# A two-layer hybrid decoder trunk on eight cores: mask, value products, MLP norm, squares and weight loads rearranged

## The reference

```python
def rmsnorm(x, g):
    y = xf * lax.rsqrt(jnp.mean(xf * xf, axis=-1, keepdims=True) + EPS)
    return (y * g.astype(jnp.float32)).astype(x.dtype)
...
        log_keep = jnp.where(mask, jax.nn.log_sigmoid(-z), 0.0)             # log(1 - beta)
        suffix = lax.cumsum(log_keep, axis=3, reverse=True) - log_keep      # sum over s<j<t
        weights = jnp.where(mask, jnp.exp(jax.nn.log_sigmoid(z) + suffix), 0.0)
        outs.append(jnp.einsum('bhqk,bhkd->bhqd', weights.astype(vb.dtype), vb))
...
    for layer in range(DEPTH):
        xn = rmsnorm(h, mix_norm_g[layer])
...
        h = h + mix
        hn = rmsnorm(h, mlp_norm_g[layer])
        h = h + jnp.square(jax.nn.relu(hn @ mlp_w1[layer])) @ mlp_w2[layer]
    return rmsnorm(h, final_norm_g)
```

## Time and profile before

| | us |
|---|---|
| median of 3 runs (lowest, highest) | 3104.32 (3099.47, 3390.04) |
| profiled execution: span of its slowest core | 3089.8 |
| spans of the 8 cores in it | 3069.8 to 3089.8 |
| PE busy, share | 2926.9, 95% |
| PE idle (span less busy) | 162.9 |
| DVE, ACT, POOL busy | 1410.4, 1412.3, 1179.8 |
| mean granted TensorE clock of the slowest core | 0.976 |

### The profile page before, as it was taken

The page is one execution under the profiler, slowest core; times in us unless marked ns, Lnnn a source line. Parts: engine busy times, 40 slices in busy tenths (PEclk is TensorE's granted clock), DMA queues, the critical chain, the costliest instruction groups (busy, mean ns, idle before and its releaser), DMA issues.

```text
span 3089.8 us, 46901 instructions; the slowest of 8 cores (3069.8 to 3089.8 us)
## 1 busy us (share of the span) xinstructions
PE 2926.9 (95%) x15157; PEld 1262.8 (41%) x15157; DVE 1410.4 (46%) x1671; ACT 1412.3 (46%) x2404; POOL 1179.8 (38%) x1685
## 2 busy tenths in 40 slices
PE   8999989999989999899998999998999989998998
PEld 3344433444433344333443444443444434443443
DVE  3410237552426445875644463333555574554002
ACT  2344243646345454356544345434554446353442
POOL 4211136343333444645443544333355435551110
PEclk9999999999999999999999999999999989999999
DMA  7788962554767998858664334465355495655222
GB/s 161 167 174 179 197 186 70 126 139 113 189 158 112 180 173 147 190 117 160 141 139 139 85 97 107 105 145 166 74 124 117 99 215 107 118 119 171 76 79 85
DMA packets 456925, 420.46 MB, mean 136 GB/s; under 512 B 310128, under 2 KB 334960, under 8 KB 456688
## 3 DMA queue, kind: packets, MB, share of 16 engines
q1 hardware_dynamic: 387424, 228.48, 32.9%
q0 software_dynamic: 69264, 188.99, 28.3%
HBM read 304.29 MB, written 89.13 MB: 127 GB/s over the span
## 4 chain that ended last, share of the span: by engine, by line
PE 80%; DVE 5%; DMA 5%; issue 3%; ACT 3%; POOL 2%; SPq 0%; DVEq 0%; ACTq 0%; POOLq 0%
PE ps L559 74%; PE ps L1282 3%; PE ps L1227 3%; DVE X_45 L674 1%; DMA Wk<-Wq 1%; DVE P L1243 1%; DMA stg<-xT 1%; DMA ring<-wblk 1%; PE ps L1231 1%; DMA h<-xT 1%; POOL ps_76 L943 1%; POOL ps_79 L943 1%; DMA oT<-stg 1%; POOL Wq L1257 1%; ACT L660 0%
## 5 line engine op out<-in xcount | busy, mean ns | idle before, releaser
L559 PE MATMUL ps<-X_45,ring 128*128 128x512 bf16 x4864 | 1118.9, 384 | 11.6 <-DVE X_45 L674 10.6
L549 ACT ACTIVATE ps<-ps 128x512 f32<-128x512 f32 (+3 forms) x832 | 576.5, 697 | 531.2 <-PE ps L559 322.5
L1257 POOL TENSOR_TENSOR Wq<-P 128x1022 bf16<-128x1022 f32 (+2 forms) x320 | 529.3, 1654 | 520.5 <-DVE P L1243 511.4
L559 PEld LDWEIGHTS ps<-X_45,ring 128*128 128x128 bf16 x4864 | 462.7, 99 | 575.9 <-issue 61.2
L1243 DVE TENSOR_TENSOR_SCAN P<-ps,carry,zeros 128x512 f32<-128x512 f32 x384 | 490.0, 1279 | 384.4 <-ACT ps L549 334.2
L559 PE MATMUL ps<-mix,ring 128*128 128x512 bf16 x2816 | 660.7, 380 | 3.6 <-DVE mix L914 2.7
L592 POOL DMA_DIRECT2D ring<-wbf x540 | 296.3, 551 | 764.9 <-PE ps L559 629.9
L715 DVE TENSOR_TENSOR h<-ps,h 128x512 f32<-128x512 f32 x384 | 263.1, 686 | 654.1 <-PE ps L559 652.3
L559 PE MATMUL ps<-ffB,ring 128*128 128x512 bf16 x2048 | 483.8, 379 | 0.0
L559 PEld LDWEIGHTS ps<-mix,ring 128*128 128x128 bf16 x2816 | 261.2, 98 | 315.4 <-issue 24.5
L1243 DVE TENSOR_TENSOR_SCAN P<-ps,zeros 128x128 f32<-128x128 f32 (+3 forms) x256 | 208.9, 820 | 375.9 <-ACT ps L549 361.7
(11 more groups left out here) (114 smaller groups left out, 1385.7 us busy)
## 6 DMA issues: line engine op xcount, KB each, us to landing
ring<-wbf POOLq DMA_DIRECT2D x540, 256.0 KB, 4.1
ring<-wblk POOLq DMA_DIRECT2D x180, 256.0 KB, 7.0
wbf<-ring SPq DMA_DIRECT2D x180, 256.0 KB, 5.7
stg<-xT SPq DMA_DIRECT2D x96, 256.0 KB, 5.4
h<-xT SPq DMA_DIRECT2D x64, 256.0 KB, 8.1
hsp<-h SPq DMA_DIRECT2D x64, 256.0 KB, 4.4
h<-hsp SPq DMA_DIRECT2D x64, 256.0 KB, 6.6
oT<-mixf SPq DMA_DIRECT2D x32, 256.0 KB, 7.6
```

The source lines that it names most:

```text
L549: return Req("act", lambda e: e.activation(out=out, in_=in_, func=func, **kw), reads, writes, dur, bias=bias)
L559: ins = pe.matmul(out, lhsT=l, rhs=r, start=(first and i == 0), stop=(last and i == n - 1), skip_group_check=True)
L1257: yield Req("pool", lambda e: e.tensor_tensor(out=W3[:, :, 0:w - 1], in0=P[:, :, 1:w], in1=P[:, :, 0:w - 1], op=ALU.subtract), [LP], [LWq] ...
```

## The change

In the code after, tensors and lines have moved: `X_45` is named `X_46`, and L559, L1227, L1282 are L588, L1349, L1402.

- **Mask.** The two mask matmuls go. The scan's second operation is max in place of add, and its second input is a floor: ones at masked places of the diagonal block, zeros elsewhere. Where the floor is one the running product stays one, and neighbouring differences are zero.
- **Value products.** Items are ordered so that four query blocks of one key chunk follow each other. Their transposes go into one buffer of 512 queries (two such buffers in place of seven small ones), and the value matmuls run once for the four: up to 512 columns each. P gets a column for the value that comes in from the right, filled by a small POOL instruction, and one subtraction makes all differences.
- **MLP norm.** `out_proj`'s result is written to X with the gain only, by DVE or ACT in turn. The sum of squares is taken aside (`rms_late`, power -1), and the second MLP matmul's result is multiplied by it on DVE and then added to h on POOL (on DVE for the last two rows of the last pass). Squared ReLU lets the scale pass as its square.
- **Squares in pairs.** Squares are written in float32 two rows at a time, a POOL or DVE add sums two rows into a bfloat16 one, and 4 ones matmuls do in place of 8.
- **Half of the first MLP matmul's squares** are made by POOL from a float32 copy in three `tmp` buffers, which frees the bank after the ReLU.
- **Weight loads** from `wbf` (540) are issued by SyncE, those from `wblk` (180) still by POOL.
- Also: three sets of conv and pool buffers in place of two, one conv step on ACT, U ahead of V in M, the gating scale and bias in one DVE instruction, `ms` buffers 4 for 2, other biases and slacks (PE no longer takes a chain's bias), attention paced at 0.4 and 0.6 of its rate in the input projections and around `out_proj` and the last second matmul, and a smaller scratch area for DMAs issued by POOL.

```diff
@@ _prep_weights, Builder.__init__, alloc
-    negq = np.where(k >= j, NEG, 0.0).astype(np.float32)
+    floor = (k >= j).astype(np.float32)
-        nc = self.nc = bass.Bass("TRN2", target_bir_lowering=False)
+        nc = self.nc = bass.Bass("TRN2", target_bir_lowering=False, dynamic_dma_scratch_size=4096)
-        self.Wk = sb("Wk", [128, NWT, 8, 128], BF16)
+        self.Wk = sb("Wk", [128, NG, 8, 512], BF16)
@@ Machine.run
-                    k = (st + f.bias + r.bias, f.n)
+                    k = (st + (r.bias if r.eng == "pe" else f.bias + r.bias), f.n)
@@ ring_fiber
-            yield Req("pool", (lambda slot, b, src: lambda e: e.dma_start(out=self.ring[:, slot, :], in_=src[b]))(slot, b, src),
+            yield Req("sp" if src is self.wbf else "pool",
+                      (lambda slot, b, src: lambda e: e.dma_start(out=self.ring[:, slot, :], in_=src[b]))(slot, b, src),
@@ new: square, rms; called by evac_x, evac_h, prefetch_x
+SQ = ((slice(0, 2), slice(2, 4), 0), (slice(4, 6), slice(6, 8), 4),
+      (slice(2, 4), slice(6, 8), 2), (slice(1, 4, 2), slice(5, 8, 2), 1))
+    def square(self, x, c, t, src, Ls, ev, eng="pool", slack=0.0):
...
+        if x == 2 and not odd:
+            yield Req("pool", lambda e: e.tensor_tensor(out=Xf[:, SQ[i][odd], hs], in0=sq, in1=sq, op=ALU.mult), Ls,
+                          [LX[k][t] for k in rows[odd]], 1.15, bias=0.5)
+        else:
+            r = self.act(Xf[:, SQ[i][odd], hs], sq, AF.Square, Ls, [LX[k][t] for k in rows[odd]], TT, False,
...
+        if odd:
+            yield lambda: c - 1 in ev.done
+            if i == 3 and x == 1:
+                eng = "dve"
+            yield Req(eng, lambda e: e.tensor_tensor(
+                out=X[:, SQ[i][2], t * TT:(t + 1) * TT].rearrange("p (a n) -> p a n", a=2),
+                in0=Xf[:, SQ[i][0], hs], in1=Xf[:, SQ[i][1], hs], op=ALU.add),
...
+    def rms(self, x, t, ev, power, parts=((0, 4),), bias=-0.05, slack=0.0):
...
+            rows = [SQ[i][2] for i in range(c0, c1)]
+            yield self.mm(self.bank(bk), [(self.cb[:, 0:128], X[:, k, ts]) for k in rows],
...
+        yield Req("act", lambda e: e.activation(out=m, in_=m, func=AF.Exp, scale=power), [], [self.Lms[ms]], 0.9)
+    def rms_late(self, t, ev):
+        self.r2[t] = yield from self.rms(2, t, ev, -1.0, bias=-0.01, slack=2.0)
@@ after out_proj: evac_x in place of evac_h and of norm_h
+            yield Req("dve", lambda e: e.tensor_tensor(out=self.h[:, c, ts], in0=self.bank(bk), in1=self.h[:, c, ts],
+                                                       op=ALU.add),
+                      [], [self.Lbank[bk], self.Lh[c][t]], 0.70)
             self.banks.free(bk)
-            if ev is not None:
-                yield self.act(self.X[1][:, c, ts], self.h[:, c, ts], AF.Square, [self.Lh[c][t]],
+            if c % 2:
+                yield Req("dve", lambda e: e.tensor_scalar(out=X[:, c, ts], in0=self.h[:, c, ts], scalar1=g, scalar2=None,
...
+            else:
+                yield Req("act", lambda e: e.activation(out=X[:, c, ts], in_=self.h[:, c, ts], func=AF.Copy, scale=g),
...
+            yield from self.square(2, c, t, self.h[:, c, ts], [self.Lh[c][t]], ev)
@@ evac_h, after the second MLP matmul
+            yield Req("dve", lambda e: e.tensor_tensor(out=self.tmp[:, b, :], in0=self.bank(bk), in1=self.ms[:, r2, :],
+                                                       op=ALU.mult),
+            self.banks.free(bk)
+            eng, d = ("dve", 0.70) if last and c >= 6 else ("pool", 1.15)
+            yield Req(eng, lambda e: e.tensor_tensor(out=self.h[:, c, ts], in0=self.tmp[:, b, :], in1=self.h[:, c, ts],
+                                                     op=ALU.add),
@@ mlp, evac1
+                if (j + t) % 2:
+                    yield self.act(m, ap, AF.Relu, [], [self.Lbank[bk], self.Ltmp[b]], TT, True)
+                    self.banks.free(bk)
+                    yield Req("pool", lambda e: e.tensor_tensor(out=F[:, jj, ts], in0=m, in1=m, op=ALU.mult),
@@ att_item
-            if first:
-                for h in range(2):
-                    ins = pe.matmul(zt[:, h * 512 + w - 128:h * 512 + w], lhsT=ident, rhs=negq, start=False, stop=True,
+        low = self.cb[:, 768 - w:768] if first else self.cb[:, 128:128 + w]
-                out=P[:, h, 0:w][:, ::-1], data0=zt[:, h * 512:h * 512 + w][:, ::-1], data1=self.zeros[:, 0:w],
-                initial=1.0 if first else self.carry[:, pv["cy"], h:h + 1], op0=ALU.mult, op1=ALU.add))(h),
+                out=P[:, h, 0:w][:, ::-1], data0=zt[:, h * 512:h * 512 + w][:, ::-1], data1=low[:, ::-1],
+                initial=1.0 if first else self.carry[:, pv["cy"], h:h + 1], op0=ALU.mult, op1=ALU.max))(h),
-        yield Req("pool", lambda e: e.tensor_tensor(out=W3[:, :, 0:w - 1], in0=P[:, :, 1:w], in1=P[:, :, 0:w - 1],
-        last = self.cf[:, 72:74] if first else self.carry[:, pv["cy"], :]
         yield Req("pool", lambda e: e.tensor_tensor(
-            out=W3[:, :, w - 1:w], in0=last.rearrange("p (h n) -> p h n", h=2), in1=P[:, :, w - 1:w], op=ALU.subtract),
+            out=W4, in0=P[:, :, 1:w + 1].rearrange("p h (j n) -> p h j n", n=128),
+            in1=P[:, :, 0:w].rearrange("p h (j n) -> p h j n", n=128), op=ALU.subtract), [LP], [LWq], w * 3.55e-3 + 0.05)
-                    ins = pe.matmul(av[h * 64:(h + 1) * 64, qc],
+        G["n"] += 1
+        if G["n"] == 4:
+                for j in range(4):
+                    q0 = j * 128 if first else 0
+                    for h in range(2):
+                        ins = pe.matmul(av[h * 64:(h + 1) * 64, q0:512],
```

442 lines of the change are left out of this document (255 added, 187 removed).

## The result

The changed kernel takes 2920.14 us (median; lowest 2914.97), the kernel before, beside it on the same chip, 3101.89 us. The ratio is 0.942, 95% interval 0.939 to 0.945: 5.8% faster, 180 us. The forecast was 2948 us.

The account below looks back on a forecast made before the run. PE bounds the kernel, busy 2926.9 of 3089.8 us. PE's work -96, waits and clock -82, new costs +22 make -156: from 3104 to 2948 us, 5% faster, range 2900 to 3000, chance 0.58.

Parts of the forecast that it names:

- PE's work, -96: Work taken from PE: value products -49 us, mask -15, ones matmuls -35, more entries into scores +3.
- Clock, -15: PE's granted clock, mean 0.976: with fewer gaps, 15 of at most 74 us lost to it come back.
- Waits that go, -67: PE's shortened waits: MLP norm 10 and 4 us, M stages 33, pool products 12, value products and scores 8.
- new ones, +22: Costs added beside PE's work: longer chain 7 us, full banks from POOL 10, late weight blocks 5.
- The MLP norm term: After `out_proj`: 10 of 11.6 us waited before `X_45,ring` go, and 4 of 16.5 before the ones matmuls.
- The longer chain, 7 us: Behind the last second-matmul group: one DVE step and a sum of rows add 1.4 us at four M starts and the end.
- POOL, 10 us: POOL's added adds, squares and sums: PE loses 10 us to full banks, bounds 0 and 75; POOL busy 1540 to 1690.
- rival B: POOL becomes the bound of evacuation, `tmp` buffers fill and PE waits for banks: 83 us more, 3031 us; chance 0.12.
- Weight loads, 5 us: 540 loads issued from SyncE: 5 us lost to late blocks, bounds 0 and 150, since the ring covers the landing.
- rival C: Weights come late, held behind transposes in SyncE's list: PE waits 243 us, 3191 us; chance 0.06.
- Rivals A and D: A: gaps nearly vanish, 2871 us, chance 0.15. D: wide pairs don't share the array, POOL costs 40 more, 3046 us, 0.09.
- The base: The forecast started from the median of 3104 us, taken as 15 us above the profiled span.

Follow-up runs that it names:

- experiment 1: Changed kernel with value products still once for four items, but in matmuls of 128 columns; ratio 0.945 to the kernel before.
- experiments 3 and 12: Both: kernel before with only the mask made a floor of the scan; no ratio, spans 3064 and 3074 us against 3087.
- the fifth experiment: Changed kernel with the norm back ahead of the MLP and the second matmul's bank added onto h by DVE at once; ratio 0.957 to the kernel before.
- experiments 4 and 8: 4: kernel before with the 540 `wbf` loads issued by SyncE alone, ratio 0.993. 8: changed kernel with these loads back on POOL, ratio 0.955.

## Why the prediction was right, step by step

**PE's work, -96.** Held where it was tested. Value groups 0.99 and 0.67 against 0.98 and 0.66, side by side (experiment 1); ones matmuls 42 (20), by the spans 26, against 35, since waits hide 9; the mask 13 to 23 by the spans of experiments 3 and 12, against 15; instructions as counted.

**Clock, -15.** The mean went from 0.976 to 0.983 on the slowest cores and 0.979 to 0.985 in the median: some 20 us. With the work that makes -116 against 129.2 of busy time measured; 13 us are not assigned. The main matmuls of `ring,X`, 512 in both, fell from 130.3 to 115.7 us busy, and they no longer stand first behind the norm; slower matmuls at M starts, paced by a row or by the clock, may be a part.

**Waits that go, -67, and new ones, +22: -45.** Idle time fell by 40.5, so the sum was right. That was luck in part: the waits that shrank gave 83 us against 67, and those that grew took 43 against 22. M stages: I left 6 us in each, measured 6.1 to 8.3; -33 was -29. Value products and scores: 19.1 and 12.4 became 0 and 6.1, 25 us, where I had put 8. The pool matmuls gave 12, as forecast. V and the gating products are part of M. **The MLP norm term missed a wait:** I took 14 us off and named as next only the copy of the last row. The first MLP matmul follows without a wait, in the two places that I read, but the ones matmuls of the late norm are queued in PE's own order and wait for POOL's squares and sums, 13.3 us. Against a kernel with the rest of the change, the deferral is worth 46 (10), by the spans 38, as the fifth experiment shows; how much of it the old schedule had hidden isn't told by it.

**The longer chain, 7 us.** `X,cbs` idles 29.8 us where all ones matmuls idled 16.5: the 13.3 us more are nearly twice the 7. The chain is multiply, POOL's add, square and sum; no run tells which step is the one that I gave too little.

**POOL, 10 us, rival B.** 1602 us lie in the forecast 1540 to 1690, and with 257 and 262 us less the kernel was 12 us slower and 6 faster by the spans. B is out, and 10 us are not contradicted. But the reason that I gave, that 45% of POOL's time is free, does not hold for all work: experiments 4 and 8 show 22 and 39 us, by the spans 24 and 29, for 296 us of issues. So 296 us of issues cost, and 260 of adds or squares hardly do, though these two runs also load DVE and ACT, which may hide a gain. What I take from the waits, and no run isolated, is the place in the order: loads come in blocks (up to eight in a row) and stand ahead of differences and sums that PE waits for. How much is their own time and how much their wait for ring slots stays open: the waits for PE were 922 us long in the kernel before and 258 in experiment 8, where the price was no smaller.

**Weight loads, 5 us, rival C.** The sign was wrong. I had costed what SyncE's queue does to loads, and nothing for what loads did to POOL's. The landing fell to 3.0, and to 2.9 with the move alone. I had worked out twice 4.1 from the h loads' 8.1 and from the Trainium skill, "DMA: Bandwidth & Descriptors", Queues, rings and completion order, which says that a DMA engine takes turns between queue rows by packets. The measurement decides: the doubling that I drew from it did not come. With this term at -22 in place of +5 the forecast would have been 2921.

**Rivals A and D.** Idle is 122 us, not 60: A is out. D needed pairs that don't share the array, and they do.

**The base.** I put the median 15 us above the span. In the changed kernel the profiled execution took 2921.85 us with a span of 2920.1, and the kernel before, beside experiment 1, 3089.89 with 3088.1. So the time outside the span is under 2 us, and the rest of the 15 was one execution differing from another. That is some 13 us of the 28 between forecast and result. The loads' sign would be 27 of it, so the two together overshoot by 12, and other terms were too good by as much. That the forecast came within 1% is owed in part to errors that cancel.

## What to carry to other kernels

Look at what an engine's list waits for before calling its work free: POOL was 38% busy and stood 922 us in front of weight loads, and moving these was worth 22 us with no work saved. But a long wait isn't a price: ask what stands behind it and whether that was ready. A group of half-array matmuls costs PE 0.12 us a turn and 0.10 an entry whatever its width, so gather items; the width itself gave nothing that the runs could tell. When a norm is deferred behind a matmul, its own ones matmuls still stand in PE's order, and their input chain has to be early.

## What was not expected of the hardware

- The loads of 256 KB landed sooner from SyncE's queue (2.9 and 3.0 us) than from POOL's (4.1, and 3.5 in experiment 8). The pages of the profile list the two queues as hardware_dynamic and software_dynamic (with the move, 228.48 MB of the first became 370.07), so issuer and kind of queue changed together.
- In experiment 5, after waits of 1.92, 2.75 and 1.08 us and matmuls 0.66 us apart, seven matmuls started 0.38 to 0.43 us apart in place of 0.216; the granted clock of these 20 us was 0.74.
- A transpose of 1.2 us (median) occupied SyncE for up to 8.8 us in the changed kernel and up to 11.2 in experiment 8.
- POOL's subtraction with four-dimensional operands lasts 1655 ns on average over all widths, where the flat one lasted 1654.
